# A deep transformer stack in one kernel: parameters fetched behind x, sums of squares inside the second panel, and half of the attention steps interleaved with the values' product

## The reference

```python
def even_mixer(h, w_in, w_out):            # layer 0: 16 heads of 64, scores masked, softmax, values
    qkv = (h @ w_in).reshape(B, S, 3, N_HEADS_EVEN, HEAD_DIM).transpose(2, 0, 3, 1, 4)
    q, k, v = rope(qkv[0]), rope(qkv[1]), qkv[2]
    ...                                    # 8 block-causal heads, 8 heads mixing three dilations
    return o @ w_out
def diff_attention(q, k, v, lam):          # layer 1: 8 heads, each the difference of two softmaxes
    ...
        s = jnp.where(kpos[None, :] <= qpos[:, None], s, -jnp.inf)
        p = jax.nn.softmax(s, axis=-1)
        a = p[:, :, 0] - lam * p[:, :, 1]
        return jnp.einsum('bhqk,bhkd->bhqd', a.astype(v.dtype), v)
x = x + even_mixer(rms_norm(x, even_norm[i]), ...)
x = x + conv_ffn(...)
x = x + diff_mixer(rms_norm(x, odd_norm[i]), ...)
x = x + conv_ffn(...)
```

## Time and profile before

| | us |
|---|---|
| median of 3 runs (range) | 3159.81 (3157.5 to 3160.11) |
| the profiled execution's own time | 3160.78 |
| its span | 3159.0 |
| PE busy | 3105.3 |
| DVE busy | 1584.0 |
| ACT busy | 1118.4 |
| mean granted clock of PE | 0.994 of full speed |

### The profile page before, as it was taken

One profiled execution on the slowest core, in us unless ns is written; L12 is line 12 of the kernel. 1 busy time (PEld: TensorE's weight loads), 2 busy tenths in 40 slices (PEclk: granted clock), 3 DMA queues, 4 the chain that ended last, 5 costly groups with the idle time before them and its releaser, 6 DMA issues.

```text
span 3159.0 us, 35038 instructions
## 1 busy us (share of the span) xinstructions
PE 3105.3 (98%) x13927; PEld 2495.2 (79%) x13932; DVE 1584.0 (50%) x2346; ACT 1118.4 (35%) x1730; POOL 20.4 (1%) x29
## 2 busy tenths in 40 slices
PE   8989999999999999999999999999999999999998
PEld 6748888887588888877788878888777888878887
DVE  5575675355566752554523463334654424453324
ACT  3254443223644432334323243322334323333322
POOL 1000000000000000000000000000000000000000
PEclk9999999999999999999999999999999999999999
DMA  5302222243022223412223223333412223223321
GB/s 189 114 8 87 100 94 97 97 140 100 1 94 94 96 98 100 139 43 93 66 95 94 94 83 102 96 94 107 121 49 78 80 94 94 88 92 99 95 94 67
DMA packets 86337, 289.30 MB, mean 92 GB/s; under 512 B 11304, under 2 KB 11320, under 8 KB 85920
## 3 DMA queue, kind: packets, MB, share of 16 engines
q1 hardware_dynamic: 83584, 278.96, 27.6%
q0 software_dynamic: 1440, 6.00, 0.5%
q10 hardware_dynamic: 1152, 2.10, 0.2%
HBM read 272.33 MB, written 2.10 MB: 87 GB/s over the span
## 4 chain that ended last, share of the span: by engine, by line
PE 94%; DVE 3%; ACT 2%; issue 1%; DMA 0%; POOL 0%; ACTq 0%; DVEq 0%; POOLq 0%
PE banks L393 74%; PE banks L455 8%; PE banks L422 3%; PE banks L729 2%; PE banks L364 1%; PE banks L533 1%; PE banks L708 1%; PE banks L502 1%; PE banks L557 1%; PE banks L545 1%; PE banks L756 0%; PE banks L782 0%; ACT prob_e L875 0%; DMA x_resid<-x_fm 0%; DVE prob_e L1396 0%
## 5 line engine op out<-in xcount | busy, mean ns | idle before, releaser
L1252 DVE TENSOR_TENSOR w_lo<-w_raw,w_hi 128x1024 fp32r<-128x1024 f32 (+1 forms) x512 | 612.4, 1207 | 915.9 <-ACT w_hi L822 914.8
L822 ACT ACTIVATE w_hi<-w_raw 128x1024 fp32r<-128x1024 f32 (+1 forms) x512 | 526.8, 1041 | 843.2 <-PE banks L393 767.3
L393 PE MATMUL banks<-h_hi,w_hi 128*128 128x512 f32 x2304 | 713.8, 391 | 10.7 <-DVE h_lo L1339 10.7
L393 PE MATMUL banks<-h_lo,w_hi 128*128 128x512 f32 x2304 | 710.7, 390 | 0.0
L393 PE MATMUL banks<-h_hi,w_lo 128*128 128x512 f32 x2304 | 710.3, 390 | 0.0
L393 PEld LDWEIGHTS banks<-h_hi,w_hi 128*128 128x128 f32 x2304 | 431.9, 188 | 100.7 <-issue 12.3
L393 PEld LDWEIGHTS banks<-h_lo,w_hi 128*128 128x128 f32 x2304 | 433.5, 188 | 90.5
L393 PEld LDWEIGHTS banks<-h_hi,w_lo 128*128 128x128 f32 x2304 | 433.4, 188 | 90.1
L393 PE MATMUL banks<-hid_hi,w_hi 128*128 128x512 f32 x668 | 206.4, 390 | 0.0
L393 PE MATMUL banks<-hid_lo,w_hi 128*128 128x512 f32 x668 | 205.8, 389 | 0.0
L393 PE MATMUL banks<-hid_hi,w_lo 128*128 128x512 f32 x668 | 205.6, 389 | 0.0
(11 more groups left out here) (278 smaller groups left out, 3170.9 us busy)
## 6 DMA issues: line engine op xcount, KB each, us to landing
w_raw<-weights SPq DMA_DIRECT2D x496, 512.0 KB, 3.6
scratch<-scratch SPq DMA_DIRECT2D x128, 64.0 KB, 2.0
w_raw<-weights SPq DMA_DIRECT2D x16, 256.0 KB, 2.6
scratch<-scratch SPq DMA_DIRECT2D x32, 128.0 KB, 2.3
x_resid<-x_fm ACTq DMA_DIRECT2D x8, 256.0 KB, 10.5
decay<-tables POOLq DMA_DIRECT2D x2, 1024.0 KB, 6.1
y_fm<-x_resid SPq DMA_DIRECT2D x8, 256.0 KB, 2.1
rope<-tables POOLq DMA_DIRECT2D x2, 512.0 KB, 4.2
```

The lines of the kernel that those rows point to most:

```text
L393: mm = e.matmul(bank[b][:, :], wt[:, k, j * P:(j + 1) * P], a[:, kt, :], start=kt == 0 and step == 0, stop=kt == k_tiles - 1 and step == 2)
L822: e.activation(m.w_hi[u % HL][:, 0:n], m.raw[u % RAW][:, 0:n], ACT.Copy).then_inc(*mark("w_hi", u))
L1252: e.tensor_tensor(m.w_lo[u % HL][:, 0:n], m.raw[u % RAW][:, 0:n], f32(m.w_hi[u % HL][:, 0:n]), ALU.subtract).then_inc(*mark("w_lo", u))
```

## The change

**Start.** ScalarE's queue issues only the first five tiles of x, SyncE's queue the other three behind the first three units of weights. GpSimd's queue holds back everything but the gains until the fifth tile of x has landed, and the parameters come after ones, identity and eps. VectorE adds the squares instead of GpSimd. The sum over the features (now one tile, `flush_tally`, 4 matmuls) is issued before k tile 2 of panel 1, the spreading before k tile 5 of panel 1. The splits of the first four units are placed elsewhere between the tiles of h and the squares.

**Attention.** 24 steps (rounds n = -1 to 4) are done beside the values' product, between its pieces of six matmuls, and the rest after it. In "e", the value product and the transpose of c = 0 come before those of c = 1. The exponentials come after the transposes' copies on ScalarE. There are six buffers of `prob` as before, two of them now over the rope table instead of h, and two of `prob_t` (in "e" four before). Beside the product there are only banks 4 to 7: in "e" 4, 5 and 6 in rotation for scores and transposes, in "d" 4 and 5 for scores and 6 for transposes and head sums; 7 for the values.

```diff
-            prob_at = [big + kb * K for kb in (48, 53, 58, 63)] + [h, h + 5 * K]
+            prob_at = [big + kb * K for kb in (48, 53, 58, 63, 78, 83)]
-            self.prob_t[st] = [at(f"probt{i}_{st}", [P, TRI_N], F32, big + (68 + 5 * i) * K) for i in range(4 if st == "e" else 2)]
+            self.prob_t[st] = [at(f"probt{i}_{st}", [P, TRI_N], F32, big + (68 + 5 * i) * K) for i in range(2)]
...
+UNDER_VALUES, LAST_UNDER = (1, 4, 4, 3, 4, 3, 3, 3), 4
+class AttentionBanks:
+    def from_pool(self):
+        self.pool += 1
+        return 4 + self.pool % 3
+    def scores(self):
+        if not self.beside_product:
+            self.pairs += 1
+            return 2 * (self.pairs % 2), 2 * (self.pairs % 2) + 1
+        return (self.from_pool(), self.from_pool()) if self.st == "e" else (4, 5)
+    def turn(self):
+        if not self.beside_product:
+            self.turns += 1
+            return 4 + self.turns % 2
+        return self.from_pool() if self.st == "e" else 6
+    def values(self, g):
+        return 7 if g <= LAST_UNDER - 2 else 6 + (g + 1) % 2
+def under_values(steps, do):
+    yield
+    for what, g, i, c in steps:
+        if what != "step_done":
+            do(what, g, i, c)
+            continue
+        yield
+        if (g, i) == (LAST_UNDER, 0):
+            return
 def attention_steps(st):
-    yield "inverse", 0, None
-    for kb in reversed(range(TB)):
-        yield "normalise", 0, kb
-    for n in range(1, DT + 3):
+    for n in range(-1, DT + 3):
         for kb in reversed(range(TB)):
             if n + 1 < DT:
-                yield "scores", n + 1, kb
-            if 2 <= n < DT + 2:
-                yield "values", n - 2, kb
-            if n <= DT:
-                yield "transpose", n - 1, kb
-            if n < DT:
+                yield "scores", n + 1, kb, None
+            for c in range(2 if st == "e" else 1):
+                if 2 <= n < DT + 2:
+                    yield "values", n - 2, kb, c
+                if 1 <= n <= DT:
+                    yield "transpose", n - 1, kb, c
+            if n + 1 < DT:
+                yield "exp", n + 1, kb, None
+            if 0 <= n < DT:
...
+            yield "step_done", n, kb, None
...
     def gemm_tm(st, hi, lo, ready, evacuated, beside, calls=None):
+                steps = calls[4 * panel + kt0 // 2] if calls else 1
...
+                        if steps > 1 and (k, pair[0]) != (1, 2):
+                            next(beside, None)
-                next(beside, None)
+                if steps in (1, 4):
+                    next(beside, None)
...
             gemm_fm("eq", DT, DT, m.h_hi, m.h_lo, ready, lambda f: ("rope_t", ("eq", f)),
-                    after_panel=lambda: (flush_squares(st), spread_for_products(st)))
+                    ahead_of={(1, 2): lambda: flush_tally(st), (1, 5): lambda: spread_for_products(st)})
...
-    for f in range(DT):
+    for f in range(X_ON_SP):
         e.dma_start(m.x[:, f, :], x_in[:, f, :]).then_inc(*mark(f"x_in{f}", 0, by=16))
...
     e.dma_start(m.par[:, 0:gains], params[:, 0:gains]).then_inc(*mark("gains_in", 0, by=16))
-    e.dma_start(m.par[:, gains:], params[:, gains:]).then_inc(*mark("params_in", 0, by=16))
+    w.wait_ge(*after(f"x_in{X_ON_SP - 1}", 0))
...
+    e.dma_start(m.par[:, gains:], params[:, gains:]).then_inc(*mark("params_in", 0, by=16))
```

More of the change, by code:

```diff
@@ L121 @@
 ON_POOL = 6
+X_ON_SP = 5
 K = 1024
@@ L517, in attention, with scores @@
         results = 2 if st == "e" else 1
[L518 to L522, removed]
+        banks = AttentionBanks(st)
+        def scores(g, i):
+            b = banks.scores()
             width = (i + 1) * P
@@ L550, in values, with transpose @@
-        def values(g, kb):
-            b, width = 6 + g % 2, P // results
-            bank_is_free(b)
[L553 to L561, removed]
+        def transpose(g, kb, c):
+            b, slot = banks.turn(), (2 * g + c) % len(prob)
+            bank_is_free(b)
+            for i in range(kb, TB):
+                w.wait_ge(*after("normed", (st, 2 * g + c, i)))
+                t = e.transpose(bank[b][:, (i - kb) * P:(i - kb + 1) * P],
+                                prob[slot][:, TRQ[i] + kb * P:TRQ[i] + (kb + 1) * P], m.ident[:, :])
+            t.then_inc(*mark("transposed", (st, g, c, kb)))
+            freed[b] = ("probt_act" if (kb + c) % 2 == 0 else "probt_dve", (st, g, c, kb))
@@ L586, in finish_heads, with do @@
             yield
[L588 to L597, removed]
-                    after_panel=lambda: (flush_squares(st), spread_for_products(st)))
[L599 to L603, removed]
         finishing = iter(())
-        for what, g, i in attention_steps(st):
+        def do(what, g, i, c):
+            nonlocal finishing
             if what == "scores":
@@ L1386, in scores @@
                 return
-            for c in range(2):
-                n, b = 2 * g + c, score_banks[2 * (turn["s"] % 2) + c]
-                width = (i + 1) * P
+            for c, b in enumerate(banks.scores()):
+                n, width = 2 * g + c, (i + 1) * P
                 w.wait_ge(*after("scores", (st, g, i, c)))
@@ L1525, in attention @@
                 scores(g, i)
-            elif what == "values" and i == 0 and st == "e":
+            elif what == "values" and i == 0 and st == "e" and c == 1:
                 values(g)
             elif what == "transpose":
-                transpose(g, i)
+                transpose(g, i, c)
             elif what == "head_squares":
@@ L1537, in attention, with beside_values @@
                 finishing = finish_heads(g, i)
+        def beside_values(steps):
+            add_swapped()
+            yield from under_values(steps, do)
+        if st == "e":
+            rope("eq", q, HD ** -0.5, None, lambda: inverse_root(st))
+        else:
+            rope("dq", q, HD ** -0.5, lambda: inverse_root(st), None)
+        rope(st + "k", k, 1.0, None, None)
+        if st == "d":
+            lambdas()
+        steps = attention_steps(st)
+        for panel in walk.tm(beside_values(steps), UNDER_VALUES):
+            for t in (0, 2):
+                w.wait_ge(*after("gemm", ("tm", st + "v", panel, t)))
+                e.tensor_scalar(v[:, t, panel * 512:(panel + 1) * 512], bank[t][:, :], stats[:, 208 + t:209 + t], None,
+                                ALU.mult).then_inc(*mark("v_dve", (st, panel, t)))
+        banks.beside_product = False
+        for what, g, i, c in steps:
+            do(what, g, i, c)
         return lambda: [None for _ in finishing]
```

269 lines of the change are left out of this document (120 added, 149 removed).

## The result

The changed kernel takes 3188.6 us (median; 3186.8 to 3193.4), the kernel before 3160.0 in the same job: a ratio of 1.0093, 95% interval 1.008 to 1.0106. It is slower by 0.9%. The forecast was 3182, the range 3155 to 3198. The profiled execution took 3187.1, its span is 3185.3 us, 26.3 longer than before.

The account below looks back on a forecast made before the run. PE, busy for 98% of the span, was taken as the bound. Start -8.0, "e" +18.0 and "d" +12.2 make +22.2 on 3160.8, giving 3183; the median 1.0 lower, 3182 us; range 3155 to 3198.

Parts of the forecast that it names:

- Start: From panel 0 to the end of panel 1: the 8.6 us gap between panels closes, -8.0 us, bounds -4 and -9.
- e: Layer "e", values' product to end of attention: 144.5 us against 126.5, +18.0, bounds +10.5 and +26.
- the lost pairs with their changes of shape: Rounds of "e": split value products each run alone, 2.13 us more a round, plus 1.3 for shape changes.
- the one at the second step: Product of "e": the second score step waits 3.0 us for a bank that DVE has not read.
- The 1.2 at the border of the panels: Product of "e": PE waits 1.2 us for bank 1, which ScalarE empties behind a step's exponentials.
- a wrong price: Score step beside the product: added window time divided by seven, 0.90 us in "e" and 0.99 in "d".
- the drain alone: Reading not chosen for "e": the new order costs only two shape changes a step, without losing the parallel half.
- d: Layer "d", values' product to end of attention: 145.6 us against 133.4, +12.2, bounds -8 and +20.
- waits for exponentials: Product of "d": scores wait until both exponentials free banks 4 and 5; longest 5.1 us, all waits 17.9.
- A: Rival, 15%: the product hides all waits, 3154 us; its turning point is two pieces between two scores.
- B: Rival, 10%: in "e" a single 128*64 product runs at twice the rate, 15 us less, 3167.
- C: Rival, 13%: repeated waits hold PE at half clock in the product, 3.4 us each; three or four give 3195.

Follow-up runs that it names:

- order_alone: The kernel before, with only the value product and transpose of c = 0 issued ahead of those of c = 1 in layer "e": 3178.6 us.
- e_pairs: The changed kernel, with both value products of layer "e" issued one behind the other, then both transposes: 3168.7 us.
- d_two_pairs: The changed kernel, with scores of the first eight steps of "d" alternating between banks 4, 5 and banks 6, 7: 3181.3 us.
- d_clock: The changed kernel, with 16, 4 and 4 dummy products ahead of the 384-column scores in rounds -1, 0 and 1 of "d": 3191.3 us.
- two_pieces: The changed kernel with 12 steps beside the product, two pieces between most, banks 4 to 7 all used, value products of "e" paired: 3145.9 us.
- two_pieces_01: The kernel two_pieces, with scores after the product beginning with banks 0 and 1 instead of 2 and 3: 3144.7 us.
- d_as_before: The changed kernel, with layer "d" in the order of the kernel before, exponentials ahead of the copies again: 3174.4 us.

## Why the prediction was right, and where it was off

**Start.** Predicted -8.0, bounds -4 and -9; -9.4 in the traces, -9.0 timed. Panel 1 ends near 35.6 instead of the 36.8 I had: panel 0 ended 1 us earlier (22.82 instead of 23.8), which I had put at nothing, the sum cost 0.81 instead of 1.05, and the spreading 0.80, not the 1.0 that I took from a row at half clock. The lower bound of -9 was too narrow.

**"e".** Predicted +18.0, measured +19.9. The term that carried it, the lost pairs with their changes of shape, was right: order_alone and e_pairs move it by 18.8 and 19.9 by themselves, with and without interleaving. I had worked out 2.13 + 1.3 a round; a round outside the product went from 9.6 to 11.8 (predicted 12.0). The product's window, to the end of its last piece, came to 99.8 (101.52 less the wait of 1.74) instead of 98, and the rest with that wait to 46.6, as predicted. That 99.8 is near 98 is in part luck: PE stands still for 4.9 us in it, where I had 6.2, and its own work took 94.8 instead of 91.7. Of the waits, the one at the second step was right (2.90, predicted 3.0). The 1.2 at the border of the panels did not come as a wait; a transpose waited that long elsewhere, for a bank of the rotation that VectorE had not read, while at the border two starts are late by 0.3 and 0.5:

```profile
132.05 0.33 PE L587 MATMUL banks<-ident,prob_e 128*128 128x128 f32 x1 [1.21 <-DVE stats L1428]
...
139.57 0.62 PE L506 MATMUL banks<-w_lo,h_hi 128*128 128x512 f32 x2
140.34 1.09 PE L506 MATMUL banks<-w_hi,h_hi 128*128 128x512 f32 x2
141.27 0.63 PE L506 MATMUL banks<-w_hi,h_lo 128*128 128x512 f32 x2
```

The work was too small because of a wrong price. I had divided what the scores add to the product's window of before by seven steps, and the window holds six; the seventh stands behind its end (timeline of PE, kernel before):

```profile
121.34 1.13 PE L533 MATMUL banks<-k_e,q_e 64*128 64x512 f32 x4
...
153.75 0.92 PE L533 MATMUL banks<-k_e,q_e 64*128 64x384 f32 x4
...
160.28 0.92 PE L533 MATMUL banks<-k_e,q_e 64*128 64x256 f32 x8
```

So a step costs 6.27 / 6 = 1.05 us in "e" and 6.93 / 6 = 1.16 in "d", not 0.90 and 0.99. By my estimate that is 2.5 to 3 us more for the 24 steps of each layer. The Trainium skill ("TensorEngine Tiling (Array Packing)", Key Properties) names both halves of the effect, parallel tiles and the drain at a change of mode. The runs give them sizes: by the drain alone order_alone would have cost some 3 us, and it cost 18.8.

**"d".** Predicted +12.2, measured +14.0 (+14.3 timed). Its two parts were each off, in opposite directions. The product's window, with 1.6 us at its end in which PE waits for banks 0 to 3, took 105.8; predicted were 100 and, in the rest, 1.8 for emptying. The waits for exponentials are there and the longest is 4.36 (predicted 5.1), but in the product's window, without the 1.6 at its end, PE stands still for 12.7 us, not 17.9. Its busy time there is 91.5 instead of the 82.0 predicted (80.5 and 1.5 for half clock). Of these 9.5, some 3.5 are the clock: three pieces at 2.7 instead of 1.36 and a slow score step cost near 5 us, and I had put 1.5. The wrong price of the score steps is nearly 3 more; what the last 3 are stays open. So two wrong terms, the waits too large and the work too small, partly cancel, and that 147.7 lies so near to 145.6 is luck. The rest took 41.9 instead of 45.6; the kernel before ran it at 0.92 of the clock and the kernel after at 1.00. Whether that is the change's doing is open. The same steps ran at 1.00 in e_pairs and d_two_pairs too, but at 0.92 in d_clock; the kernels with the old order in "d" had 0.89 to 0.96 there.

**The rivals.** *A* is refuted: the product hides little of it with one piece between scores. Its turning point was right, though: two_pieces puts two pieces there, PE's waits for exponentials are gone from the product of "d" (in two_pieces_01 only 0.8 us are left, behind the product), and the loss with them, though no gain of "d" is shown. *B* is refuted by order_alone. *C* happened in part: half clock behind three waits of "d", with some 5 us lost rather than 12; the dense pieces between the waits did not by themselves hold the clock up. d_clock shows that holding the clock up there by dummy products gives nothing that can be measured.

**Why 3182 and not 3188.6.** The profiled execution took 3187.1: the parts add up to 22.2 in the forecast and to 24.5 in the traces, and 1.8 came from the layers that the change leaves alone. The other 2.5 is that execution's place among the runs, which spread over 6.7 us: the median lies 1.5 above it, and I had put it 1.0 below.

## What to carry to other kernels

Before you reorder matmuls that use half of the array each, look in the timeline whether two of them start together; what one costs is then what both cost, and a matmul of the full array put between them doubles it. When small steps are laid between pieces of a dense product, compare the longest chain from a result to its freed bank with the work between two steps. Here 2.74 us stood against 1.36, and "d" lost 14; a second pair of banks in its first eight steps gave back half of that. With twice the work between the steps and the banks 4 to 7 all in use the loss was gone, and "e" gained. And when a price is a difference divided by a count, count the instructions in the window. A part of a change is worth timing alone: this one held -9 and +34.

## What the runs showed of the hardware

The same wait may or may not cost the clock. Stage e has the same instructions in the kernels after, d_as_before, d_two_pairs and d_clock, and took 146.4, 149.4, 152.3 and 152.4 us. Behind the wait of 1.74 us at the end of the product, the kernel after goes on at full clock (the scores of 384 columns at 204.85 took 0.85 to the next start), while d_clock, behind the same 1.74, drops to half (1.58; PE's timeline of d_clock):

```profile
205.16 1.13 PE L580 MATMUL banks<-k_e,q_e 64*128 64x512 f32 x4 [1.74 <-DVE v_e L1558]
...
208.01 1.65 PE L580 MATMUL banks<-k_e,q_e 64*128 64x384 f32 x4
209.59 1.11 PE L600 MATMUL banks<-probt_e,v_e 128*64 128x256 f32 x2
```

Its window from there to the end of the attention:

```profile
205.16:254.46 49.30, 48.42 (x193) 19.58 (x193) 24.60 (x82) 18.16 (x52) 0.00 (x0) 0.90 0.00 1
```

That costs 4.4 us of this window (49.30 against 44.89). Nor does the length of the wait alone decide: in the kernel after, the wait of 2.90 us in "e" left the clock at 1.00, while in "d" half clock followed waits of 1.17 and 0.44 (769.55 and 770.22). This kernel, with its many waits of one to five microseconds between matmuls, so has not one time but a spread: a stage of one profiled execution is known to some 6 us here, and a difference of that size between two traces of such a stage is not yet an effect of an edit.
